# Four products of the identity ahead of the second ffn_up chunk

## The reference

```python
def conv_ffn(h, w_up, conv_w, conv_b, w_down, rows, cols):
    z = (h @ w_up).reshape(b, rows, cols, 2 * D_FF)
    z = lax.conv_general_dilated(z, conv_w[:, :, None, :], window_strides=(1, 1), padding='SAME', ...)
    z = z.reshape(b, l, 2 * D_FF) + conv_b
    return (jax.nn.silu(z[..., :D_FF]) * z[..., D_FF:]) @ w_down

x = x + mx[:, :, 5] * conv_ffn(h2, ffn_up, ffn_conv_w, ffn_conv_b, ffn_down, rows, GRID_W)
return rmsnorm(x, final_g)
```

## Time and profile before

| what | us |
|---|---|
| median of 3 runs | 745.47 |
| lowest and highest of them | 740.64 and 749.41 |
| the profiled execution's own time | 743.66 |
| its span, first to last instruction | 741.8 |
| TensorE busy in it | 718.3 |

### The profile page before, as it was taken

One profiled execution on the slowest core, in us unless ns is written; L12 is line 12 of the kernel. 1 busy time (PEld: TensorE's weight loads), 2 busy tenths in 40 slices (PEclk: granted clock), 3 DMA queues, 4 the chain that ended last, 5 costly groups with the idle time before them and its releaser, 6 DMA issues.

```text
span 741.8 us, 14168 instructions
## 1 busy us (share of the span) xinstructions
PE 718.3 (97%) x5844; PEld 695.2 (94%) x5844; DVE 496.1 (67%) x905; ACT 360.5 (49%) x459; POOL 402.3 (54%) x223
## 2 busy tenths in 40 slices
PE   6899999999999989999999999999999899999998
PEld 3798789999999989999999999999999899999997
DVE  3877797669536569877777774558865465566663
ACT  6688134245444456555555546445554344334331
POOL 0776544556549957888878887766795400000000
PEclk9999999999999989999999999999999999999999
DMA  9994888337534537455555554433435545655611
GB/s 359 419 397 162 339 287 310 143 114 262 204 114 160 175 125 300 174 192 205 174 175 193 201 171 171 159 127 114 171 115 195 202 160 182 228 175 172 222 57 57
DMA packets 21089, 145.84 MB, mean 197 GB/s; under 512 B 2465, under 2 KB 2977, under 8 KB 3746
## 3 DMA queue, kind: packets, MB, share of 16 engines
q1 hardware_dynamic: 20880, 144.87, 53.9%
q10 hardware_dynamic: 146, 0.07, 0.0%
HBM read 143.88 MB, written 1.05 MB: 195 GB/s over the span
## 4 chain that ended last, share of the span: by engine, by line
PE 87%; DVE 3%; DMA 3%; ACT 3%; issue 2%; POOL 1%; DVEq 0%; ACTq 0%; POOLq 0%
PE bank L1434 23%; PE bank L1435 22%; PE bank L1436 22%; PE bank L1452 5%; DMA raw<-in_w_in 3%; PE CP L1435 2%; PE CP L1434 2%; PE CP L1436 2%; PE bank L1544 2%; ACT whi L490 1%; POOL wlo L463 1%; DVE H4l L1380 1%; PE bank L1477 1%; DVE GA L1137 1%; PE bank L1492 1%
## 5 line engine op out<-in xcount | busy, mean ns | idle before, releaser
L469 POOL TENSOR_TENSOR wlo<-raw,whi 128x512 fp32r<-128x512 f32 (+1 forms) x189 | 366.5, 1970 | 153.1 <-ACT whi L487 153.0
L487 ACT ACTIVATE whi<-raw 128x2048 fp32r<-128x2048 f32 x100 | 190.8, 1909 | 59.9 <-DMA raw<-in_w_in 32.3
L1204 DVE SCALAR_TENSOR_TENSOR Y<-bank,vec,Y 128x189 f32<-128x189 f32 (+2 forms) x352 | 123.0, 422 | 40.4 <-ACT Y L739 40.3
L1434 PE MATMUL bank<-H2h,whi 128*128 128x256 f32 x352 | 100.1, 284 | 1.7 <-DVE H2l L1179 1.7
L1435 PE MATMUL bank<-H2l,whi 128*128 128x256 f32 x352 | 100.0, 284 | 0.0
L1436 PE MATMUL bank<-H2h,wlo 128*128 128x256 f32 x352 | 99.9, 284 | 0.0
L1434 PE MATMUL bank<-H1h,whi 128*128 128x256 f32 (+1 forms) x288 | 90.0, 312 | 4.8 <-DVE H1l L931 1.9
L1436 PE MATMUL bank<-H1h,wlo 128*128 128x256 f32 (+1 forms) x288 | 88.3, 307 | 0.0
L1435 PE MATMUL bank<-H1l,whi 128*128 128x256 f32 (+1 forms) x288 | 88.2, 306 | 0.0
L864 DVE TENSOR_TENSOR wlo<-raw,whi 128x2048 fp32r<-128x2048 f32 x28 | 64.6, 2307 | 31.0 <-ACT whi L487 31.0
L1434 PE MATMUL bank<-H4h,whi 128*128 128x256 f32 x256 | 71.8, 280 | 2.4 <-ACT whi L487 2.4
(11 more groups left out here) (327 smaller groups left out, 1899.9 us busy)
## 6 DMA issues: line engine op xcount, KB each, us to landing
raw<-in_w_mlp SPq DMA_DIRECT2D x32, 1024.0 KB, 4.9
raw<-in_w_in SPq DMA_DIRECT2D x30, 1024.0 KB, 6.5
raw<-in_ffn_up SPq DMA_DIRECT2D x22, 1024.0 KB, 4.9
raw<-in_ada_hi SPq DMA_DIRECT2D x16, 1024.0 KB, 5.5
raw<-in_ffn_down SPq DMA_DIRECT2D x11, 1024.0 KB, 4.8
raw<-in_w_out SPq DMA_DIRECT2D x8, 1024.0 KB, 4.9
ada_s<-in_ada_s SPq DMA_DIRECT2D x4, 1024.0 KB, 17.9
ada_p<-in_ada_p SPq DMA_DIRECT2D x2, 1024.0 KB, 10.1
```

The lines of the kernel that those rows point to most:

```text
L469: m = e.tensor_tensor(l[:, a:a + step], r[:, a:a + step], h[:, a:a + step].bitcast(F32), ALU.subtract)
L487: e.activation(whi[q % NHI][:, :], raw[n % NRAW][:, :], ACT.Copy).then_inc(s["w_hi"], 1)
L1204: e.scalar_tensor_tensor(o[:, r0:r1, c0:c1], z[:, r0 + dr:r1 + dr, c0 + dc:c1 + dc], cw[:, f, tap:tap + 1], o[:, r0:r1, c0:c1], ALU.mult, ...
L1434: e.matmul(out, h[:, col:col + P], xh, start=first, stop=False, skip_group_check=True)
```

## The change

`pair` gets a parameter `settle`. Where it is set, four products of the identity with itself are issued behind the waits for weights and bank, each into 128 columns of the bank that the chunk is about to fill. It is set for the second chunk of ffn_up alone. The chunk's own matmuls then start the bank anew.

```diff
-        def pair(name, i, xh, xl, ks=range(KT), ready=None, apart=False, midway=None):
+        def pair(name, i, xh, xl, ks=range(KT), ready=None, apart=False, midway=None, settle=False):
             h, l = weights(name, i)
             bs = [group(name, i), group(name, i, 1)] if apart else [group(name, i)] * 2
+            if settle:
+                for n in range(4):
+                    e.matmul(bs[0][:, n * P:(n + 1) * P], ident, ident, start=True, stop=True)
...
-                pair("ffn_up", i, H2h, H2l, ready=h2_ready if i == 0 else None)
+                pair("ffn_up", i, H2h, H2l, ready=h2_ready if i == 0 else None, settle=i == 1)
```

## The result

| what | kernel before | changed kernel |
|---|---|---|
| median | 743.22 us (20 runs) | 745.85 us (20 runs) |
| lowest and highest | 737.40 and 749.56 | 738.65 and 752.54 |
| runs under 743 us | 10 of 20 | 1 of 20 |
| the profiled execution's own time | 743.66 | 750.60 |

The ratio is 1.005, with a 95% interval of 1.0027 to 1.0073: the change makes the kernel 0.5% slower. The ratio leaves out, on both sides, the runs over 1.5% above the fastest of their kernel (four of each twenty); the two medians of the table, over all runs, are 0.35% apart. The forecast was 740.3 us, 0.7% faster. The time lies in the range given, and within 1% of before, but on the other side of it.

What follows compares the result with a forecast made beforehand. TensorE, busy 97% of 741.8 us, was taken as the bound. 6.1 us gained by faster matmuls less 0.9 us for the products gives 5.2 us: 745.47 - 5.2 = 740.3 us, range 735.5 to 748.0 us.

Steps and rivals of the forecast that it cites:

- The two paces: TensorE's 256-column matmuls: 113.3 or 117.8 ns each, 0.218 us per group of 48, 7.0 us over 32 groups.
- The products' own time: Four products ahead of the second ffn_up chunk cost 0.90 us on TensorE, unhidden; bounds 0.80 and 1.05 us.
- The end of the stretch: Before w_in_2: TensorE 6.1 us ahead, 0.9 us lost to a longer wait, some 1.5 us; everything behind 5.2 us earlier.
- a pace is drawn behind a wait: On TensorE, after a wait the pace is drawn anew and falls either way, slow or fast.
- rival two: Last MLP, behind its wait, falls slow and costs 6.0 us: 746.3 us by the median; chance 0.15.
- I take it that the stream leaves them fast: Behind the four products at the second ffn_up chunk TensorE runs at 113.3 instead of 117.8 ns, worth 7.0 us.
- twelve places: Places behind at least four 128-column fp32 products where the 256-column stream came out fast; three had been slow just before.
- the pace ahead of the products: TensorE's stream from 270 us, second half of the first ffn_up chunk, was taken as slow, 117.8 ns.
- -5.2 us: Forecast net change at the start of w_in_2: 6.1 us gained up to the 21st ffn_up chunk, less 0.9 us.
- Rival three: TensorE waits at the eighth ffn_up chunk, slow from there; only 0.6 us gained, 744.9 us by the median; chance 0.08.
- The 0.6 us at the eighth chunk: Margin at the eighth ffn_up chunk: weights ready at 311.1 us, as before, TensorE there at 311.7 us.
- Rivals one and two: Rival one: products at the second ffn_up chunk don't turn the pace, only cost 0.9 us: 746.4 us by the median; chance 0.17.

Runs made afterwards that it cites:

- the repeat: A second trace of the changed kernel, with nothing changed against it: 744.71 us.
- the faster execution of before: The kernel before, unchanged, run once more for a second trace: 739.36 us.

## Why the prediction was wrong

**What held.** The two paces, 113.3 and 117.8 ns, and their worth: from the first matmul behind the products to the last of ffn_down it is 454.23 - 273.36 = 180.87 us in the repeat, and 446.91 - 272.65 = 174.26 us in the faster execution of before. The difference is 6.6 us; 32 x 0.218 us less the wait of 0.19 us at the eighth chunk makes 6.8 us. The products' own time: in the timeline of after, 275.00 - 273.88 = 1.12 us where two fast steps take 0.23 us, so 0.89 us (0.90 forecast from the earlier trace rows). The end of the stretch: a fast stream does meet a longer wait ahead of w_in_2 (1.50 us, as forecast), and a slow one comes there as in the earlier trace rows. Also that a pace is drawn behind a wait, that rival two's last MLP can fall slow, and what that costs (6.0 us forecast, 5.9 to 6.0 us measured): it was slow in two of the three traces of the changed kernel, fast in both of before, and slow in three of the twelve others. Nothing ties it to the change, and so few traces don't exclude it either.

**The step that failed** is "I take it that the stream leaves them fast". It rested on twelve places, put together as one kind and read only by what came out of them. What the runs showed in its place: an even number of these products turns the pace over, an odd number keeps it. The rows had it. Each of the places with the identity fits: the earlier trace rows four products, slow to fast (and eight near 215 us, slow to fast); of the earlier trace rows, which I read as "once slow and once fast", both are even sets that turned the pace: the one at 564.90 us had a slow stream ahead of it, the one at 53.79 us a fast one. Had I written the pace ahead beside the pace behind for these two, the rule would have been a rival with a chance. The other ten of the twelve places are products with another moving operand (the levels, L1544, and what follows them), nine of them with a fast stream ahead. There the forecast's reading, fast behind, holds; it doesn't carry over to the identity. Why the two kinds differ stays open; no run was made on it.

**The second fault** was to take the pace ahead of the products from one execution. It had been slow at the end of the first chunk, and from there turning over would have been the gain forecast. But that is the rarer draw: in 17 traces of these kernels, whose first chunks are alike, the stream ends the first chunk fast in 12. From a fast stream the change costs. In place of -5.2 us, the repeat against the faster execution of before shows +5.35 us.

**Rival three** was right as a mechanism, and the margin set against it was wrong. The 0.6 us at the eighth chunk rested on "a backlog that starts with the first chunk's results, which the change doesn't move". That is so in the kernel before. With products at the second chunk VectorE waits for that chunk too, and the backlog starts there and moves with them. In the one trace with the forecast's own case, slow turned to fast at the second chunk, TensorE did wait at the eighth (311.93 to 312.25 us): no margin was left. A stream fast from the first chunk waits there as well, 0.19 to 0.20 us, in the kernel before and with three and with five products; only products put in the wait's own place took it away. Behind it the stream was fast in one such trace and slow in two. In the kernel before this gives a part of the fast executions back.

**Does this give the size?** An estimate, in terms of the start of w_in_2. From a fast stream the changed kernel stands at 455.17 us. Before stands at 448.68 us if the eighth chunk stays fast, and near 453.57 - 0.67 = 452.90 us if it falls slow (the trace with three products less their time): 6.5 or 2.3 us worse, 4.4 us at half each. From a slow stream, by the prediction's own sums, it is 5.2 or 0.6 us better, 2.9 us at half each. With 12 and 5 of 17 that is 12/17 x 4.4 - 5/17 x 2.9 = 2.3 us slower. Measured are 2.6 us between the medians, 3.7 us by the ratio, and 2.0 to 5.4 us by its interval. It fits at the low end, but the shares are from few traces. It was not shown how often each draw falls: a kernel with a controlled first draw would be needed.

The range held because the scatter of the draws was put into it; 0.60 went to a case that comes only from a slow first chunk (5 of 17 traces), 0.17 to one that one even set of 94 may have shown (products that don't turn the pace), and the case that came most often, a turn to slow, had none. Rivals one and two come nearest by their number (746.4 and 746.3 us, measured 745.85 us); that is luck, since neither describes what happened in the repeat.

## What to carry to other kernels

Where the same instructions run at two paces, write for each border both the pace ahead and the pace behind; "always fast behind" and "turned over" look alike as long as only slow streams are looked at. A single execution shows one draw of such a state, so an edit that acts on the state is to be costed from each state, with its share. A margin of some tenths of a microsecond at a wait holds only if the row that starts the backlog is found, not just a window in which the engine is full, and if the change opens no new wait behind that row.

## What the runs showed of the hardware that was not expected

At a granted clock of 1.00 a stream of 128x128 blocks times 256 columns runs at 113.3 or 117.8 ns a matmul, and holds the slow pace for 181 us and the fast one for 136 us without a change (the stretches above from 273.36 and from 310.93 us). An even number of plain fp32 products of 128 columns between them, with the identity as the moving operand, exchanges the two paces and an odd number doesn't: 115 of 116 sets, with 1 to 16 products, and with three kinds of stationary operand, and 66 of 68 places of the kernel's own. With other moving operands a fast stream stayed fast behind 8 and 16 products at all 153 places. Each product is two records, so the number of records is even in both cases, and that it is even can't be what decides; what does, the profile doesn't show. All products take the same time, so a rule by their number and one by the length of the set can't be told apart. Such a product costs 0.223 to 0.224 us.

A wait of 0.19 us is enough to throw the pace open. These draws can make most of the scatter of one and the same kernel: the 20 runs of before lie in three heaps, near 738, 743 and 749 us (6, 9 and 5 of them), the stretch to w_in_2 is worth 6.5 us, and the pace of the last MLP 6.0 us. Which of the 20 runs drew what is not on record.

The Trainium skill (TensorE: Matmul & The Clock Gate, Back-to-back issue gap) gives an isolated step of columns over 2.4 GHz and 2.5 ns; by that an estimate for 256 columns is 109.2 ns. The same section limits this: in a stream of weight loads and matmuls both set the step, 81 ns for 128 columns and 131 ns for 512. The prediction left this limit out. The paces of this stream, 113.3 and 117.8 ns for 256 columns, lie 4 and 9 ns above the isolated step and between the two figures for a stream, and the section names no second pace.
